# Two networks in one launch: the norms between stages without their multiplications of the unit matrix

## The reference, cut to what matters

```python
def rms_norm(x, g):
    xf = x.astype(jnp.float32)
    y = xf * lax.rsqrt(jnp.mean(xf * xf, axis=-1, keepdims=True) + RMS_EPS)
    return (y * g.astype(jnp.float32)).astype(x.dtype)

def mod_norm(x, m, i, g):
    return rms_norm(x, g) * (1 + m[:, 3 * i + 1, None]) + m[:, 3 * i, None]

def ffn_sublayer(x, m, i, g, w1, w2):
    return x + HALF_STEP * m[:, 3 * i + 2, None] * swiglu(mod_norm(x, m, i, g), w1, w2)
```

## Time and profile before

| | |
|---|---|
| median of 3 runs | 2800.92 us |
| lowest and highest | 2800.55 and 2805.89 us |
| the profiled execution | 2799.17 us |
| its span | 2797.3 us |
| mean granted TensorE clock | 0.994 |
| TensorE busy | 2732.1 us, 98% of the span |
| VectorE, ScalarE, GpSimd busy | 2067.0, 1216.9 and 522.2 us |
| moved by DMA | 462.50 MB, mean 165 GB/s |

### The profile page before, as it was taken

One profiled execution on the slowest core, in us unless ns is written; L12 is line 12 of the kernel. 1 busy time (PEld: TensorE's weight loads), 2 busy tenths in 40 slices (PEclk: granted clock), 3 DMA queues, 4 the chain that ended last, 5 costly groups with the idle time before them and its releaser, 6 DMA issues.

```text
span 2797.3 us, 40204 instructions
## 1 busy us (share of the span) xinstructions
PE 2732.1 (98%) x15618; PEld 2320.2 (83%) x15618; DVE 2067.0 (74%) x3773; ACT 1216.9 (44%) x2228; POOL 522.2 (19%) x449
## 2 busy tenths in 40 slices
PE   7999999999999999999988999999999999999998
PEld 5888878668888878888885999889999888888887
DVE  6989895568989896564766766765896677777776
ACT  5323233453232342222445545565556444444444
POOL 1111114300111101010050000345898000000000
PEclk9999999999999999999999999999999999999999
DMA  7555533223555445354441566424654556655554
GB/s 290 194 186 192 185 136 112 76 103 123 202 182 190 175 154 189 122 191 145 146 148 45 191 216 216 146 84 151 197 152 121 185 190 192 192 193 190 190 190 132
DMA packets 123261, 462.50 MB, mean 165 GB/s; under 512 B 13504, under 2 KB 26688, under 8 KB 109888
## 3 DMA queue, kind: packets, MB, share of 16 engines
q1 hardware_dynamic: 109248, 359.27, 39.5%
q0 software_dynamic: 13824, 100.67, 9.3%
HBM read 452.93 MB, written 6.95 MB: 164 GB/s over the span
## 4 chain that ended last, share of the span: by engine, by line
PE 90%; DVE 7%; issue 1%; ACT 1%; DMA 1%; POOL 1%; POOLq 0%; DVEq 0%; ACTq 0%
PE bank L283 28%; PE bank L284 27%; PE bank L285 27%; PE bank L2469 2%; DVE weight_lo L182 1%; DVE extension_ffn L920 1%; DVE nmax L1397 1%; DMA extension_ffn<-in_w_mods 1%; DVE arena L544 1%; PE bank L940 1%; PE bank L941 1%; PE bank L385 0%; PE bank L508 0%; DVE extension_mixer L1390 0%; POOL weight_lo L235 0%
## 5 line engine op out<-in xcount | busy, mean ns | idle before, releaser
L175 ACT ACTIVATE weight_hi<-weight_ring 128x512 fp32r<-128x512 f32 x1272 | 798.7, 631 | 1188.2 <-PE bank L285 1187.1
L182 DVE TENSOR_TENSOR weight_lo<-weight_ring,weight_hi 128x512 fp32r<-128x512 f32 x1110 | 839.4, 760 | 430.6 <-ACT weight_hi L175 428.9
L283 PE MATMUL bank<-operand_hi,weight_hi 128*128 128x256 f32 (+1 forms) x3168 | 1045.4, 330 | 16.8 <-DVE operand_lo L561 5.6
L284 PE MATMUL bank<-operand_lo,weight_hi 128*128 128x256 f32 (+1 forms) x3168 | 1032.8, 326 | 0.0
L285 PE MATMUL bank<-operand_hi,weight_lo 128*128 128x256 f32 (+1 forms) x3168 | 1032.6, 326 | 0.0
L283 PEld LDWEIGHTS bank<-operand_hi,weight_hi 128*128 128x128 f32 x3168 | 602.2, 190 | 86.1 <-issue 16.1
L284 PEld LDWEIGHTS bank<-operand_lo,weight_hi 128*128 128x128 f32 x3168 | 602.6, 190 | 53.1 <-issue 0.5
L285 PEld LDWEIGHTS bank<-operand_hi,weight_lo 128*128 128x128 f32 x3168 | 602.1, 190 | 50.4
L920 DVE SCALAR_TENSOR_TENSOR extension_ffn<-extension_ffn,silu_c 128x512 f32<-128x512 f32 x532 | 388.4, 779 | 1.7
L235 POOL TENSOR_TENSOR weight_lo<-weight_ring,weight_hi 128x512 fp32r<-128x512 f32 x162 | 211.6, 1315 | 421.1 <-ACT weight_hi L175 418.3
L283 PE MATMUL bank<-hidden_hi_ffn,weight_hi 128*128 128x512 f32 (+1 forms) x704 | 256.6, 364 | 4.0 <-DVE arena L1173 4.0
(11 more groups left out here) (280 smaller groups left out, 2543.5 us busy)
## 6 DMA issues: line engine op xcount, KB each, us to landing
weight_ring<-in_ffn SPq DMA_DIRECT2D x272, 512.0 KB, 3.5
weight_ring<-in_experts SPq DMA_DIRECT2D x256, 512.0 KB, 3.5
extension_ffn<-in_w_mods POOLq DMA_DIRECT2D x96, 1024.0 KB, 7.6
weight_ring<-in_w_mix SPq DMA_DIRECT2D x56, 512.0 KB, 3.4
weight_ring<-in_w_second SPq DMA_DIRECT2D x52, 512.0 KB, 3.6
spill<-early_retrieve SPq DMA_DIRECT2D x45, 128.0 KB, 3.9
arena<-spill SPq DMA_DIRECT2D x45, 128.0 KB, 3.5
extension_mixer<-in_rel_bias SPq DMA_DIRECT2D x2, 1536.0 KB, 6.7
```

The costliest lines, as they stand in the source:

```text
L175: nc.scalar.activation(self.hi[:, g % 2, h], self.ring[:, g % NS, h], ACT.Copy).then_inc(self.rounded, 1)
L182: self.nc.vector.tensor_tensor(self.lo[:, g % 2, h], self.ring[:, g % NS, h], self.hi[:, g % 2, h].bitcast(F32), ALU.subtract).then_inc(se ...
L283: nc.tensor.matmul(out, a_hi, b_hi, start=start and n == 0, stop=False)
L284: nc.tensor.matmul(out, a_hi, b_lo, start=False, stop=False)
```

## The change

The calls of `keep_warm` are taken out of `Norm.sums`, `Norm.spread`, `DoubleNorm.sums` and `DoubleNorm.spread`. The method itself stays, with no caller. Nothing else is changed: no wait, no buffer, no transfer, and no instruction of another engine.

```diff
@@ -501,8 +501,6 @@
             if kt == 0 and not self.by_sums:
                 pe.wait_ge(self.gathered.sem, self.gathered.at(KT - 2))
             else:
-                if not self.by_sums:
-                    c.keep_warm(pe, self.spare, 3)
                 pe.wait_ge(self.squared.sem, self.squared.at(kt + 1))
@@ -523,15 +521,11 @@
         c, nc, n = self.chip, self.chip.nc, self.blocks
-        if not self.by_sums:
-            c.keep_warm(pe, self.spare, 2)
         pe.wait_ge(self.inverted.sem, self.inverted.at(1))
         for b in range(n):
             last = nc.tensor.matmul(c.bank[7][:, b * P:(b + 1) * P], c.rstd4[:, b:b + 1].to_broadcast([P, P]), c.ident[:, :],
                                     start=True, stop=True)
         last.then_inc(self.rstd_there.sem, 1)
-        if not self.by_sums:
-            c.keep_warm(pe, self.spare, 8)
@@ -603,7 +597,6 @@
     def sums(self, pe):
-        self.chip.keep_warm(pe, self.spare, 5)
         self.sum(pe, KT - 1)
@@ -627,13 +620,11 @@
     def spread(self, pe):
         c, nc = self.chip, self.chip.nc
-        c.keep_warm(pe, self.spare, 6)
         pe.wait_ge(self.inverted.sem, self.inverted.at(1))
         for b in (2, 3, 0, 1):
             last = nc.tensor.matmul(c.bank[7][:, b * P:(b + 1) * P], c.rstd4[:, b:b + 1].to_broadcast([P, P]), c.ident[:, :],
                                     start=True, stop=True)
         last.then_inc(self.rstd_there.sem, 1)
-        c.keep_warm(pe, self.spare, 7)
```

## The result

| | before | after |
|---|---|---|
| median | 2800.8 us (20 runs) | 2807.09 us (20 runs) |
| lowest and highest | 2797.67 and 2805.89 | 2804.87 and 2809.28 |
| profiled execution, its span | 2799.17, 2797.3 us | 2807.38, 2805.6 us |
| mean granted TensorE clock | 0.994 | 0.985 |

The kernel is slower by 6.3 us: the ratio is 1.0021, with a 95% interval of 1.0014 to 1.0028. That is inside the range forecast (2797.5 to 2809.0) and above the forecast of 2802.3. It lies nearest to the slower rival's 2808.1. The mean clock shows the same in all the runs, not only in the profiled one: it is 0.984 or 0.985 in each of the 20 after, and 0.992 to 0.995 in the 60 runs of before that were taken with the experiments.

A forecast was written before the change was run, and what follows sets the result against it. TensorE, busy for 98% of the span, was taken as the bound. 2.6 us won against 4.0 lost to clock dips made it 1.4 us slower, a median of 2802.3 us; range 2797.5 to 2809 us.

The forecast's parts named there:

- slower rival: A second dip follows on the next stage's first matmuls, from three such places on; four give 2808.1 us; chance 0.22.
- The gains: Earlier last sums at places 1, 3, 4 (0.54 us each) and 7 (0.7), earlier double-norm spread (0.3): 2.6 us won.
- the clock falls at all seven places: Between one stage's last matmul and the next's first, without turns, a dip comes at seven places instead of three.
- One dip of 3.4 us at each of the seven places: At each stretch between stages, one 3.4 us fall to half clock and no second one; 4.0 us lost in sum.
- The sum: Dips cost 0.91 us at places 2 and 4, 0.9 at 5 to 7, less 0.5 at 7: 4.0 lost against 2.6 won.
- The price of half clock: A dip costs 0.91 us on the 8-matmul spread, 0.9 on 256-wide pairs, nothing on 512-wide; second dip: 2.3 and 1.5.
- The rule of the Trainium skill: TensorE left idle between bursts starts each one cold; by it alone seven new dips and a median of 2805.0 us.
- What the text said would show it: Earlier sums and double-norm spread, 3.4 us dips nearly everywhere, spread 1.16 or 2.07 us, matmuls 0.21 us apart at places 5-7.
- three signs of being wrong: Places 2, 4, 5, 6 still at clock 1.00; 6.8 us dips with slow stages, past 2806 us; time changing outside the places.

The follow-up runs named there:

- placed kernel: Against the kernel before: fewer turns ahead of late sums and the double norm's spread, more in TensorE's waits; 2797.87 us against 2800.05, again 2798.47 against 2801.01.

## Why the prediction was right or wrong, point by point

**The number and the mechanism.** 2807.09 us lies in the range because the range was drawn to take in the slower rival. The forecast itself was 1.4 us of loss, and 6.3 came.

**The gains** (2.6 us) were in the main read rightly. The last sums at place 3 start right behind the first ones, the double norm's spread starts at 1760.64, 0.05 us behind its reciprocal's end, and the removal of the turns ahead alone brought 0.5 us at places 1 and 3 and 0.8 at place 7, against 0.54 and 0.7 forecast. At place 7 one was missed. The turns behind the spread were put at nothing, but there the spread ended at 1921.03, the first operand takes 1.73 us from the spread's end (by the trace after), and the pair started at 1923.56, 0.8 us later than that: at half clock the eight turns stood in its way. The placed kernel won this too, among its 1.65 us.

**That the clock falls at all seven places** came true in the profiled execution, where three of seven had dips before.

**"One dip of 3.4 us at each of the seven places" is the step that failed.** Every dip took 6.8 or 10.2 us, and 3.7 to 5.1 us of it lay on the next stage's matmuls. The sum had 2.7 us for dips on the pairs (0.9 at each of places 5 to 7, nothing at 1 to 4); by the account they cost 7.5 us (5.2 at 5 to 7, 2.3 at 1 to 3). I had this as the slower rival, at 0.22, and held against it that every mid-kernel dip of the trace lasted 3.4 us. But at the places those dips had the eight turns behind the spread inside them, and with only these taken out the dips at places 1, 3 and 7 last 10.2 us. The evidence against the rival was made by the very instructions that the change removes; I had written that down as the point for it and gave it too little weight.

**The price of half clock** was nearly right. The spread costs 0.9 us more (2.08 against 1.16). Place 1 of the placed kernel was profiled once with the dip and once without, and won 0.2 and 1.1 us against before, 0.9 us apart. The 256-wide pairs were put at 0.9 us for one dip and 2.3 for two, and cost 1.3, 1.7 and 2.2 us with 4.5 to 5.1 us of the pair at half clock. The 512-wide ones were put at nothing and 1.5 us, and cost 0.5 to 1.0 us with 3.7 to 4.8. Place 4, with narrow matmuls at the wide pace of VectorE, cost nothing behind the place, as worked out.

**Where the gains lie against the price.** Places 1 and 3, which had their dip before, are faster after the change by 0.7 and 0.6 us; the others, place 4 and above all 2, 5, 6 and 7, are slower. The sum had the dip stay on the spread at places 1 and 3. In this execution it came later, and the two spreads won 0.8 and 0.9 us that nobody forecast. That is luck of the execution: with the same counts, the kernel with all turns out at places 1 to 4 had a spread of 1.96 us at place 1 and lost 0.9 us there.

**The rule of the Trainium skill** (TensorE: Matmul & The Clock Gate, its section on HAM oscillation): idling between bursts makes each start cold. The change bears it out as to the outcome, with seven cold starts. The run with 2-column turns shows that it isn't idling as the profile counts it: the engine was busy for 5.70 of 5.70 us at 0.50.

**What the text said would show it** was there: the sums and the double norm's spread as early as forecast, first matmuls at half speed at places 5 to 7 (0.21 us apart). Of the three signs of being wrong that it names, the second is what happened: dips of 6.8 us and more, slow starts behind them, and a time past 2806. The third, time that changes outside the places, is in the profiled execution too (2.6 us), and is of the kind that comes and goes.

**Left open:** which executions have a dip at which place. The same place of the same kernel shows both, and no run here controls it. Nor was it tried how few turns behind the spread would do. The account by place rests on one execution of each kernel.

## What to carry to other kernels

Filler work for the clock has two jobs, to prevent a fall and to end one, and in this kernel the second was worth more (4.5 us against nothing measurable): put it between the last small operation and the start of the next dense stage. Before taking such work out, look at the dips that are left while it is there; their length is not what they would be without it. Fill the waits that the trace shows, with matmuls as wide as the ones that were seen to help (128 columns here), and keep filler out from ahead of a step that is already ready, where it costs its own duration (0.4 to 0.5 us at three places here).

## What the runs showed of the hardware that I had not expected

A matmul of 2 columns with a 128 x 128 stationary operand costs as much time as one of 128 columns (0.213 us from start to start at half clock, 0.112 us at full clock, for both). With 2-column turns the clock fell at all seven places, as with no turns. It stayed at 0.50 for 13.7 us at place 7 of that kernel, while the profile has TensorE busy for all of them:

```profile
1929.10:1942.80 13.70, 13.70 (x66) 13.70 (x66) 6.93 (x18) 4.85 (x10) 0.54 (x1) 0.50 0.31 116
```

Whether the clock falls at a borderline place differs between executions of one kernel, and a dip on the spread is 0.9 us. With seven such places and a few more in the mixers, this can make up a good part of the spread of the runs of before (2797.67 to 2805.89 us). The 60 runs of before taken with the experiments bear it out: the 11 with a mean clock of 0.995 took 2798.1 us in the mean, and the 4 with 0.992 took 2805.2. That it makes up all of the spread is not shown.
